# Router logits taken from the residual with scaled router weights, and transposes mixed with the shared expert's gate, in a two-layer mixture-of-experts step

## The reference

```python
def rmsnorm(x, gain):
    return x * lax.rsqrt(jnp.mean(x * x, axis=-1, keepdims=True) + NORM_EPS) * gain

def trunk_layer(x, cond, lw, ...):
    mod = silu(cond) @ w_ada + b_ada              # shift1, scale1, gate1, shift2, scale2, gate2
    ...
    x = x + gate1 * (mix @ w_out)
    h = rmsnorm(x, norm_ffn) * (1 + scale2) + shift2
    x = x + gate2 * moe_ffn(h, lw)

def moe_ffn(x, lw):                               # T = 256 tokens, 1024 wide
    scores = sigmoid(x @ router_w)                # 64 experts
    ...                                           # best 4 of 8 groups, then best 6 experts, gates
    routed = moe_dispatch(x, eidx, gates, exp_w_gate, exp_w_up, exp_w_down)
    shared = (silu(x @ sh_w_gate) * (x @ sh_w_up)) @ sh_w_down
    return routed + shared
```

## Time and profile before

| | before |
|---|---|
| median of 3 runs | 1344.55 us (1344.04 to 1345.78) |
| the profiled execution | 1345.73 us |
| its span, first to last instruction | 1343.9 us |
| PE busy | 1235.8 us (92%) |
| DVE busy | 273.3 us (20%) |
| ACT busy | 236.1 us (18%) |
| HBM read | 493.60 MB, 369 GB/s over the span |

### The profile page before, as it was taken

How to read it: one execution, slowest core, us unless ns; L and a number is a source line. 1 busy time by engine, 2 the same in 40 slices (tenths; PEclk the granted TensorE clock), 3 DMA queues, 4 the chain that set the end, 5 groups by cost and what they waited for, 6 DMA issues and landing times.

```text
span 1343.9 us, 22748 instructions
## 1 busy us (share of the span) xinstructions
PE 1235.8 (92%) x9612; PEld 838.9 (62%) x9612; DVE 273.3 (20%) x714; ACT 236.1 (18%) x521; POOL 2.8 (0%) x13
## 2 busy tenths in 40 slices
PE   6999999999998889888999999999999889888986
PEld 4566687667755566556565668866767565556554
DVE  1253342110111010101034424411011010101012
ACT  2363131110010001000134431311010001000102
POOL 0000000000000000000000000000000000000000
PEclk8999999999999899889999999999999899899989
DMA  9879849999999999999956663999999999999992
GB/s 385 323 316 346 348 190 410 383 422 420 420 420 422 422 422 422 422 422 422 402 201 264 244 242 152 415 383 422 422 420 421 421 421 422 422 422 422 422 419 85
DMA packets 80657, 496.58 MB, mean 369 GB/s; under 512 B 10576, under 2 KB 12880, under 8 KB 24784
## 3 DMA queue, kind: packets, MB, share of 16 engines
q1 hardware_dynamic: 76528, 493.63, 89.7%
q10 hardware_dynamic: 4064, 2.00, 0.5%
HBM read 493.60 MB, written 2.00 MB: 369 GB/s over the span
## 4 chain that ended last, share of the span: by engine, by line
PE 71%; DMA 23%; DVE 2%; issue 1%; SPq 1%; ACT 1%; DVEq 0%; ACTq 0%
DMA dn<-in_exp_w_down 19%; PE PS L2147 15%; PE PS L2183 13%; PE PS L2077 8%; PE PS L2084 7%; PE PS L1649 7%; PE PS L1981 4%; DMA gu<-in_exp_w_gate 3%; PE PS L1573 2%; PE PS L2043 2%; PE PS L1605 2%; DMA gu<-in_w_in 1%; PE PS L1772 1%; PE PS L1783 1%; PE PS L2123 1%
## 5 line engine op out<-in xcount | busy, mean ns | idle before, releaser
L2147 PE MATMUL PS<-gu,arena 128*32 128x256 f32 (+1 forms) x3072 | 316.6, 381 | 0.0
L2183 PE MATMUL PS<-arena 128*64 128x512 f32 (+1 forms) x336 | 177.9, 679 | 62.1 <-DMA dn<-in_exp_w_down 60.6
L2147 PEld LDWEIGHTS PS<-gu,arena 128*32 128x32 f32 (+1 forms) x3072 | 183.9, 118 | 79.0 <-issue 18.0
L2183 PE MATMUL PS<-dn,arena 128*32 128x512 f32 (+1 forms) x688 | 185.6, 637 | 0.0
L2077 PE MATMUL PS<-arena 128*128 128x128 f32 x1408 | 176.3, 278 | 0.5 <-ACT arena L1023 0.5
L2077 PEld LDWEIGHTS PS<-arena 128*128 128x128 f32 x1408 | 164.1, 192 | 17.9 <-issue 16.7
L2084 PE MATMUL PS<-arena 128*128 128x256 f32 x704 | 160.2, 380 | 1.4 <-ACT arena L1006 1.4
L2147 PE MATMUL PS<-arena 128*64 128x256 f32 (+1 forms) x672 | 152.0, 379 | 0.0
L2084 PEld LDWEIGHTS PS<-arena 128*128 128x128 f32 x704 | 130.2, 190 | 20.5 <-ACT arena L1006 3.2
L1484 DVE TENSOR_TENSOR arena<-arena,PS 128x256 f32<-128x256 f32 x44 | 18.5, 422 | 563.7 <-ACT arena L1019 563.7
L1006 ACT ACTIVATE arena<-PS 128x512 f32<-128x512 f32 x88 | 52.6, 597 | 459.0 <-PE PS L2183 459.0
(11 more groups left out here) (257 smaller groups left out, 1022.9 us busy)
## 6 DMA issues: line engine op xcount, KB each, us to landing
gu<-in_exp_w_gate SPq DMA_DIRECT2D x106, 1024.0 KB, 16.5
gu<-in_exp_w_up SPq DMA_DIRECT2D x86, 1024.0 KB, 17.6
dn<-in_exp_w_down SPq DMA_DIRECT2D x86, 1024.0 KB, 18.1
arena<-in_exp_w_up SPq DMA_DIRECT2D x42, 1024.0 KB, 14.9
arena<-in_exp_w_down SPq DMA_DIRECT2D x42, 1024.0 KB, 16.7
gu<-in_w_ada SPq DMA_DIRECT2D x20, 2048.0 KB, 8.8
xh<-in_exp_w_gate SPq DMA_DIRECT2D x22, 1024.0 KB, 11.3
gu<-in_w_in SPq DMA_DIRECT2D x8, 2048.0 KB, 13.1
```

The lines of the kernel that those rows point to most:

```text
L2147: ins = mmul(PS[w * h:w * h + w, 5, FF * half:FF * half + FF], xg[:, k, w * h:w * h + w], weights[half][:, k], start=(k == 0), stop=(k == ...
L2183: ins = mmul(PS[w * h:w * h + w, 7 - n, :], hidT[:, j * P + w * h:j * P + w * h + w], weights[:, j, 512 * n:512 * n + 512], start=(j == 0) ...
```

## The change

The logits are `h @ W` with `h = x * r * a + s`, where `r` is the norm factor of a token, `a` the norm's gain times one plus the scale, and `s` the shift. The new kernel computes them as `r * (x @ (a W)) + s @ W`. DVE forms `a W` for both token groups (`scaled_rt`) and the products of `s` and `W`, reduced over the chunks (`shift_sum`), before the last attention results arrive; one matmul with ones sums `shift_sum` over the partitions. The router's matmuls then read `xT` and stand where the filler matmuls stood. DVE combines factor, product and shift (`logits_ready`) after the third modulated chunk. ACT, which had token group 0 of all chunks and now has both groups from chunk 3 on, loads the sigmoid's table before its first chunk and applies the sigmoid after its third. PE, in place of router, all transposes and then the gate's first half, takes chunk by chunk two transposes and the shared gate's matmuls. The computation of `amp` moves from the end of the residual additions to before the new products. In the first norm of layer 0 one semaphore is dropped.

```diff
+        SECOND_D = 3
@@ ACT, norm(k), second norm of a layer
+                if k % 2:
+                    A(small[:, 501:502], col("eps"), ACT.Sigmoid)
                 for c in range(NC_):
...
                     act.wait_ge(S["xn_ready"], NC_ * k + c + 1)
-                    A(hT[:, c, 0:P], xn[:, c, 0:P], ACT.Identity, scale=amp[:, w, c, 0:1],
-                      bias=mod[:, l, 3 * w, c, 0:1]).then_inc(S["h_a"], 1)
+                    for g in range(2 if k % 2 and c >= SECOND_D else 1):
+                        ins = A(hT[:, c, g * P:g * P + P], xn[:, c, g * P:g * P + P], ACT.Identity, scale=amp[:, w, c, g:g + 1],
+                                bias=mod[:, l, 3 * w, c, g:g + 1])
+                    ins.then_inc(S["h_a"], 1)
+                    if k % 2 and c == SECOND_D - 1:
+                        act.wait_ge(S["logits_ready"], l + 1)
+                        A(score, score, ACT.Sigmoid).then_inc(S["sig_exp"], 1)
...
-                act.wait_ge(S["router_done"], l + 1)
-                A(score, PS[:, 4, 0:G * E].rearrange("p (g e) -> p g e", g=G), ACT.Sigmoid).then_inc(S["sig_exp"], 1)
@@ DVE, norm(k)
                     v.reciprocal(small[:, G:2 * G], small[:, 0:G]).then_inc(S["rstd_ready"], 1)
+                    link(v.tensor_copy(shift_sum, PS[:, 2, 0:G * E]))
...
+                if k % 2:
+                    normed(0)
+                    for c in range(SECOND_D):
+                        normed(c + 1)
+                        modulated(c)
+                    v.wait_ge(S["router_done"], l + 1)
+                    for g in range(G):
+                        ins = stt(score[:, g], PS[:, 4, g * E:g * E + E], small[:, G + g:G + g + 1],
+                                  shift_sum[:, g * E:g * E + E], ALU.mult, ALU.add)
+                    ins.then_inc(S["logits_ready"], 1)
+                    for c in range(SECOND_D + 1, NC_):
+                        normed(c)
+                    return
@@ DVE, before the residual additions
                 ada(ADA_BY[l] - 1)
+                amplify(2 * l + 1)
...
                 v.tensor_copy(dk_tok, PS[:, 2, 256:512]).then_inc(S["ktok_ready"], 1)
+                v.wait_ge(S["router_in"], 16 * (l + 1))
+                router = w_rt.rearrange("p (c e) -> p c e", c=NC_)
+                for g in range(G):
+                    tt(scaled_rt[:, g], router, bc(amp[:, 1, :, g], 2, E), ALU.mult)
+                tt(shift_rt[:, 0], router, bc(mod[:, l, 3, :, 0], 2, E), ALU.mult)
                 v.wait_ge(S["t_mix"], 2 * l + 2)
                 v.tensor_copy(mixT[:, 0:2, :], PS[:, 5, :].rearrange("p (k t) -> p k t", k=2)).then_inc(S["mixT_d"], 1)
                 settle("mixT_d")
+                link(tt(shift_rt[:, 1], router, bc(mod[:, l, 3, :, 1], 2, E), ALU.mult))
+                v.tensor_reduce(shift_sum.rearrange("p (g e) -> p g e", g=G), shift_rt.rearrange("p g c e -> p g e c"), AX.X,
+                                ALU.add).then_inc(S["router_scaled"], 1)
...
-                amplify(2 * l + 1)
                 add_squares(STEPS[0][-1], True)
@@ PE, norm(k)
-                fill(2, bank=5)
+                pe.wait_ge(S["x_bank"], x_steps(2 * l) + 1)
+                pe.wait_ge(S["router_scaled"], l + 1)
+                mmul(PS[:, 2, 0:G * E], C("ones"), shift_sum, start=True, stop=True)
+                routed(range(4))
...
-                fill(1)
+                routed(range(4, 6))
...
-                fill(2)
+                routed(range(6, NC_)).then_inc(S["router_done"], 1)
@@ PE, after norm(2 * l + 1)
-                for k in range(NC_):
...
-                        ins = mmul(PS[:, 4, g * E:g * E + E], hT[:, k, g * P:g * P + P], w_rt[:, k * E:k * E + E],
...
-                for g in range(G):
-                    for c in range(NC_):
+                for c in range(NC_):
+                    pe.wait_ge(S["h_a"], NC_ * (2 * l + 1) + c + 1)
+                    pe.wait_ge(S["h_d"], h_d_count(2 * l + 1, c))
+                    for g in range(G):
                         ins = turn(PS[:, 2 * g + c // 4, (c % 4) * P:(c % 4) * P + P], hT[:, c, g * P:g * P + P])
...
-                shared_part(6, 0, 0, range(NC_))
+                    if c < NC_ - 1:
+                        shared_part(6, 0, 0, (c,), first=(c == 0))
+                    if c < 4:
+                        shared_part(6, 0, 1, (c,), first=False)
...
-                shared_part(6, 0, 1, range(4))
+                shared_part(6, 0, 0, (NC_ - 1,))
```

More of the change, by code:

```diff
@@ L403, in trunk @@
             cond_ready caches_placed
-            tables_in chunk_r chunk_sel chunk_mod chunk_amp ada_r ada_sel ada_mod
+            tables_in chunk_r chunk_sel chunk_amp ada_r ada_sel ada_mod
             sq_ready sq_summed ss_ready std_ready rstd_ready rstd_spread xn_ready h_a h_d amp_ready
@@ L1125, in norm @@
                         v.wait_ge(S["chunk_sel"], c // 2 + 1)
-                        told = ("chunk_mod", c // 2 + 1) if c < NC_ - 2 else ("ada_mod", 1)
-                        tt(mod[:, 0, 0:2, c:c + 2], PS[:, 6, 0:8].rearrange("p (s c g) -> p s c g", s=2, g=G),
-                           bc(b_ada[:, 0, 0:2, c:c + 2], 3, G), ALU.add).then_inc(S[told[0]], 1)
-                        v.wait_ge(S[told[0]], told[1])
+                        ins = tt(mod[:, 0, 0:2, c:c + 2], PS[:, 6, 0:8].rearrange("p (s c g) -> p s c g", s=2, g=G),
+                                 bc(b_ada[:, 0, 0:2, c:c + 2], 3, G), ALU.add)
+                        if c < NC_ - 2:
+                            link(ins)
+                        else:
+                            ins.then_inc(S["ada_mod"], 1)
+                            v.wait_ge(S["ada_mod"], 1)
                         stt(amp[:, 0, c:c + 2], mod[:, 0, 1, c:c + 2], 1.0, bc(gains[:, 0, c:c + 2], 2, G), ALU.add,
@@ L1627, in norm, with routed @@
                     return
-                fill(2, bank=5)
-                pe.wait_ge(S["sq_summed"], k // 2 + 1)
+                l = k // 2
+                def routed(cs):
+                    for c in cs:
+                        pe.wait_ge(S["x_bank"], x_steps(2 * l) + [c in step for step in STEPS[0]].index(True) + 1)
+                        for g in range(G):
+                            ins = mmul(PS[:, 4, g * E:g * E + E], xT[:, c, g * P:g * P + P], scaled_rt[:, g, c],
+                                       start=(c == 0 and g == 0), stop=(c == NC_ - 1), skip_group_check=True)
+                    return ins
+                pe.wait_ge(S["x_bank"], x_steps(2 * l) + 1)
+                pe.wait_ge(S["router_scaled"], l + 1)
+                mmul(PS[:, 2, 0:G * E], C("ones"), shift_sum, start=True, stop=True)
+                routed(range(4))
+                pe.wait_ge(S["sq_summed"], l + 1)
                 for g in range(G):
@@ L1756, in chunks_select @@
                         if i > 0:
-                            pe.wait_ge(S["chunk_mod"], i)
+                            pe.wait_ge(S["chunk_amp"], i)
                         for n in range(4):
@@ L2023, in _, with shared_part @@
                 norm(2 * l + 1)
[L2026 to L2046 removed]
+                w = piece(("shared", l, 0)).rearrange("p (u k t j) -> p u k j t", u=2, k=NC_, j=2)
+                def shared_part(bank, u, j, ks, first=None):
+                    for k in ks:
+                        ins = mmul(PS[:, bank, j * T:j * T + T], w[:, u, k, j], hT[:, k, :],
+                                   start=(k == 0 if first is None else first), stop=(k == NC_ - 1), skip_group_check=True)
+                    return ins
+                for c in range(NC_):
+                    pe.wait_ge(S["h_a"], NC_ * (2 * l + 1) + c + 1)
+                    pe.wait_ge(S["h_d"], h_d_count(2 * l + 1, c))
+                    for g in range(G):
+                        ins = turn(PS[:, 2 * g + c // 4, (c % 4) * P:(c % 4) * P + P], hT[:, c, g * P:g * P + P])
+                        if c == NC_ - 1:
+                            ins.then_inc(S["t_h"], 1)
+                    if c < NC_ - 1:
+                        shared_part(6, 0, 0, (c,), first=(c == 0))
+                    if c < 4:
+                        shared_part(6, 0, 1, (c,), first=False)
                 pe.wait_ge(S["routed"], l + 1)
```

25 lines of the change are left out of this document (9 added, 16 removed).

## The result

The changed kernel takes 1337.85 us (median of 5 runs, 1336.18 to 1338.24) against 1345.34 of the kernel before beside it (5 runs, 1344.04 to 1346.57): ratio 0.9943, 95% interval 0.9929 to 0.9956. A second set of five gave 1337.90 and 0.9951 (0.9938 to 0.9965). Over all runs of this study before is at 1344.8 (median of 112 runs) and after at 1337.9 (10 runs): 7.0 us. The profiled execution of after took 1338.24.

What follows compares the result with a forecast made beforehand. Weights at 420 to 422 GB/s pace the expert halves, so an earlier PE pays only through stream holes. Layer gains 2.4 + 1.9 = 4.3 us bring 1345.73 to 1341.4, as a median 1340.3; range 1338.8 to 1343.4.

Steps and rivals of the forecast that it cites:

- the shift: Transition before the experts, each layer: counts and first round start 2.4 us earlier, with ends 1.6 and 2.6.
- the step from shift to time in layer 1: Layer 1's hole lacks 2.0 us by bytes, 1.4 by share, less than the 2.4 head start; gain taken as 1.9.
- Router ahead of the norm: PE after `w_out`: 18 matmul halves at 0.108 us (or 0.128), 1.94 us; first normed chunk at 191.75 or 192.2.
- DVE up to the choice: DVE's normed chunks, modulations and logit steps (0.4 us): choice of experts starts at 195.6 instead of 198.12, 2.5 us earlier.
- ACT: After the sigmoid, ten modulations at 0.49 us each end at 199.5, last transposes at 200.0; no extra 1.38 us after table load.
- rival A: ACT's ten modulations or slow router matmuls decide: shift 1.6 us in both layers, 3.2 in all, 1341.4 us; chance 0.14.
- PE will stand for about 1.3 us where it was busy, at no cost, as the ranks come from DVE: Between counts and ranks: three shared-gate matmuls fewer there leave PE idle about 1.3 us, at no cost.
- Work before the residual additions: New products (0.69 us each) and a reduction (1.4, or 2.8) fit idle stretches of 3.10 and 3.74 us; cost at most 0.3.
- The fourth fixed expert: Its load is issued about 3 us later, behind seven 1 MB loads lasting 17.5 us; the weight stream doesn't notice.
- From shift to time, layer 0: Weight stream's hole in layer 0, missing 2.9 us of bytes: the whole 2.4 shift is gained and 1.3 us of hole remain.
- B: Early expert rounds wait for their own weights: layer 1 gives nothing, layer 0 about 2.0 us, 1342.5 us; chance 0.13.
- C: Without fillers PE falls to 1.2 GHz in the transition: net 1.0 us slower in each layer, 1346.6 us; chance 0.06.

Runs made afterwards that it cites:

- e11: Changed kernel with a 2.9 us DVE delay before the choice of experts in layer 1 only, PE's wait filled with three fillers: 1342.27 us, ratio 0.9981 to before.
- e15: Changed kernel with a 2.9 us DVE delay before the choice of experts in layer 0 only, PE's wait filled with three fillers: 1342.03 us, ratio 0.9979 to before.
- e10: Changed kernel with a 2.9 us DVE delay before the choice of experts in both layers, PE's wait filled with three fillers: 1345.27 us, ratio 1.0001 to before.
- e13: The kernel before, unaltered, run for a second trace: 1344.51 us.
- e14: The kernel before, unaltered, run for one more trace: 1350.04 us.
- e17: Changed kernel with PE's transposes and shared gate in the old order, six fillers in PE's wait for the chunks: 1347.34 us, ratio 1.0015 to before.
- e12: Kernel before with each chunk's transposes moved right behind its router matmuls, router after the norm and shared gate unchanged: 1346.00 us, ratio 1.0007 to before.
- e4: Changed kernel with the semaphore chunk_mod restored in the first norm: 1337.53 us beside 1337.90 for the changed kernel.
- e16: Changed kernel with one filler matmul in PE's wait before the ranks' matmul, both layers: 1338.50 us, ratio 0.9943.
- e9: Changed kernel with five fillers in PE's loop before the down matmuls of every pair round of turns 3 to 8, no code copied out: 1337.39 us.
- e6: Changed kernel with a 2.9 us DVE delay before the choice of experts in layer 0 only, PE's wait left unfilled: 1341.33 us.
- e5: Changed kernel with five fillers before the down matmuls of the last long-wait pair round, that turn copied out of PE's loop: 1343.02 us.
- e1: The changed kernel, unaltered, run for a second trace: 1337.90 us.

## Why the prediction was off

The direction was right, and so was the path up to the first round. The time, 1340.3 (1338.8 to 1343.4), was 2.5 us too high, and the result lies under the range. Two steps failed: the shift, put at 2.4 with 2.6 as its upper end, was 2.9 in each layer, and the step from shift to time in layer 1, which capped the gain at 1.9 by the hole's missing bytes. The second is the larger.

- *Router ahead of the norm*: right. 16 halves take 1.90 us, 0.119 each, between the two prices. The first normed chunk starts 3.9 us after `w_out` (predicted 4.0).
- *DVE up to the choice*: right, 2.66 us earlier (2.5). The two logit steps take 0.47 (0.4).
- *ACT*: the table load ends at 190.50 and the next activation starts at 190.52, in the timeline above. The Trainium skill (ScalarE: Activation LUTs, What ACT_TABLE_LOAD costs) has a further 1.38 us there; the trace doesn't. Ten modulations take 3.94 us, not the 4.9 that the mean of 491 ns gave. Their mean duration here is 478 ns, so they overlap by 93 ns each, which is what the same section of the Trainium skill states. That cleared away rival A. The counts follow the choice with nothing lost (2.67 earlier), and I had cut 0.1 for it.
- *"PE will stand for about 1.3 us where it was busy, at no cost, as the ranks come from DVE"*: half wrong, and one of the failed steps. PE did stand (1.00), but before, the ranks' matmul had been PE's: four shared gate matmuls ran from 203.91 on, 2.00 us, and L2062 followed them at 205.85 without a wait. After, it waits for DVE. This gave 0.24 more. With 2.67 at the counts the shift is 2.9 instead of 2.4, beyond my end of 2.6. The two lines of the kernel before:

```profile
203.91 2.00 PE L2043 MATMUL PS<-xh,gu 128*128 128x256 f32 x8
...
205.85 0.27 PE L2062 MATMUL PS<-arena,cst 64*2 64x64 f32 x2
```

- *Work before the residual additions*: hidden. The reduction took 1.92 us for 1.4, and DVE still waited 1.06 us for PE behind it. The fourth fixed expert was loaded 1.9 us later, counted from `w_out`, not 3, and the stream did not notice.
- *From shift to time, layer 0*: the hole shrank to (66 + 103 + 12) x 2 / 422 = 0.9 us, with 0.7 behind it at 250 to 256 us; 1.3 was forecast. By bytes moved 100 us behind the start of C the stream gained 2.1 us between the first traces, and 2.0 to 3.4 over the four traces of before's code and four of after's. The 2.4 of the forecast lies among them. By the time, the head start in layer 0 alone gave 2.8 (e11).
- *Layer 1*: this step failed. I took 1.9, since the hole misses only 2.0 us of bytes and "the rest of the head start is spent waiting for weights". By the time the head start in layer 1 was worth 3.05 us alone (e15 against before; the interval, 1.6 to 4.2, still holds 1.9) and 4.4 on top of layer 0's (after against e11); taking back both cost 7.4 (e10), where the forecast had 4.3 for both. Why it is more than the hole's bytes stays open. The second dip of 1.1 us would fill the sum, but it stands in one of three traces of before only. Against e13 and e14 the stream leads by 2.0 us 100 us behind the start of D, as I had counted, and yet PE leads by 2.4 at its last long wait for down weights and by 3.3 to 4.5 at the end, all counted from the start of D. So a part of the gain comes up behind that wait, and no view names its cause. (The lead of 5.7 us that bytes moved show between the first traces from 912 us on holds 1.2 us from A and the second dip.)
- With shifts of 2.9 in full in both layers the sum would be 5.8 and the forecast 1338.7 as a median. The remaining 1.2 us (7.0 in all runs) are not explained. Against the kernel before beside them, e10, e11, e15, e17 and e12 all differ by what their first rounds are earlier or later in both layers, to within 0.4 us (0.2 for 0.0, -2.8 and -3.05 for -2.9, 2.3 for 2.1, 0.9 for 0.6; stretches at the lower clock are left out of the first rounds). The kernels with both head starts (after, e4, e16, e9) are 0.8 to 1.9 us faster than by this sum, and e6 3.6 us. What I can name are stretches that vary within one code: B in two of five traces, T (31.1 in all traces of unaltered after code, 31.1 to 32.1 in before's), M, the clock dips. None is shown to be the cause.
- *Rivals*: B did not occur; no wait for weights stands in the first three rounds. C did not in the first profiled run of after, but in 4 of 16 traced layers with its transition a small form of it did, 1.4 to 1.6 us each, which would be about 0.8 us per run on average. I had excluded it with one wait of 2.0 us at full clock; one row is no bound.

## What to carry to other kernels

The missing bytes of a hole are no upper bound for what a head start in front of it is worth: here the hole of layer 1 missed 2.0 us, and a head start of 2.9 us was worth 3.05 alone and 4.4 on top of the other layer's. Keep the whole shift inside the range, and settle it by taking the shift back in one layer at a time. Trace each kernel more than once before a difference between two traces is given a cause; the second dip behind the hole and 2 us of E were in one trace only. When two edits meet at one instruction (here the counts), ask what each gives without the other; here neither form that was tried gave anything. And a delay put in to measure a path must keep PE busy meanwhile, or it measures the clock.

## What the runs showed of the hardware

- A PE wait of 3.22 us before the counts doubled the price of a 2.9 us delay (6.25 us at the first round), because PE worked at 1.2 GHz behind it (clock 0.50 for about 10 us from 200 us on).
- PE stood up to 4.15 us for "issue" where a loop's body had been copied out behind the loop (e5), and 3.13 us before `w_out` in one of the runs of before (e14). No view names what it waited for.
- The long waits for down weights end 12.4 us after the load's issue in both kernels (1268.84 to 1281.21, 1275.53 to 1287.88). But for the first one of a layer, which can be shorter (3.49 in e1), all last 5.2 us: the round of two waits at the same point of a cycle of 44.7 us, in before as in after.
- In each of the two kernels' first traces 14 of 20 loads of an ACT table are followed by the next activation within 0.01 us; the other six stand before longer waits.
